# An attention and expert-retrieval block: x of 16 tokens copied earlier, five rounds of row gathers ahead of the scatter, gates stored in quarters

## The chip, the cores and the metric

The kernel runs on one core of a Trainium2 chip. A core has TensorE (PE; its weight loads are PEld), VectorE (DVE), ScalarE (ACT), GpSimd (POOL), the SP sequencer that only issues DMAs here, and 16 DMA engines. Every engine runs its own program in order, and the programs meet at semaphores. The metric is the device time of one execution in microseconds (us); less is better.

## The reference

One block of 512 tokens of width 1024, all in float32:

```
z   = x @ w_in                       # attention: two groups of 8 heads
x1  = layer_norm(ALPHA * x + concat(fox(z), swa(z)) @ w_out)
q   = x1 @ w_pq                      # 8 heads, two halves of 128
v1, i1 = top16(q_a . keys1);  v2, i2 = top16(q_b . keys2)
sc, pos = top16(all 256 sums v1 + v2)      # 16 experts a head of 128 * 128
gate = softmax(sc);  e = i1 * 128 + i2
w   = gelu(u_tab[e] . x1) * gate           # 8 heads * 16 = 128 experts a token
out = layer_norm(ALPHA * x1 + sum(w * v_tab[e]))
```

## The kernel before

**Precision.** A float32 product is made of three passes of rounded parts: hi*hi, lo*hi and hi*lo. Each 128 x 1024 tile of a table is loaded into one of four `raw` slots by SP, rounded to `hi` by ScalarE (`split_hi`, L446), and the rest is made by GpSimd (`split_lo`, L452). There are four such pairs for expert tiles. SP loads tile c + 4 only when the `lo` of tile c is made.

**Tokens.** The 512 tokens are four blocks of 128. Blocks 1 to 3 (384 columns, `DENSE`) are computed densely: TensorE multiplies x1 with all 128 tiles of u (L1806 to L1808), ScalarE takes the gelu (L1018), the result is stored to DRAM as `gelu_scratch` (L557), the last 12 tiles being kept on chip. Then weights = gelu * gate enter the products with the 128 tiles of v (L1861 to L1863). Block 0 is done by gathers: GpSimd gathers for each of 128 ranks the row of u of every token (L765) and VectorE takes the dot with x1 (L1347). The dots run against a copy of x in PSUM, `x1_home`, that ScalarE writes with `home` (L1047). Eight ranks make a round; there are eight row buffers, so rank k is gathered only when the dot of rank k - 8 is done (`row_used`). The last 16 tokens of block 3 are also left out of the dense u product (368 columns): their 16 * 128 rows are spread over all 128 partitions as 16 more ranks, the "late" ones. For these, SP copies numbers (L580), gates (L587) and x (L592) of the 16 tokens across partitions, eight DMAs each, and later brings the weights back (L598).

**The route.** VectorE finds the chosen experts block by block (`route_block`), with dots in the gaps (`DOT_GAPS`), 28 in all; after the gate sums it does dots until `R_PRE` rounds of eight are done (`while done[0] < R_PRE * ROWS`), then casts the gates and begins the one-hots.

**The scatter.** The gates of the dense tokens must be laid out by expert. For eight tokens at a time VectorE makes one-hot rows (L1570, L1577, L1578), TensorE multiplies them (L2078, L2079) and ScalarE copies the result to one of two `stage` buffers (L1060). A chunk is 32 tokens, four such groups, six u tiles; `two_chunks(o)` covers twelve u tiles, and there are six of them, o = 0 to 5. Ahead of them are 44 u tiles (`A_PRE`, numbers 0 to 43), behind them 12. After the sixth and the twelfth tile of a pair SP stores a whole stage buffer (2 MB, L610), and ScalarE waits for that store (`g_stored`) before it writes the buffer again. In the first pair the scatters stand after tiles 2 to 5 (numbers 46 to 49) and then after each (0, 1, 3, 4) of six.

**Orders that the change touches.** ScalarE, first pair: gelu of tile 44, `take_turned`, gelu of tile 45, wait for the copies of x and for `R_PRE * ROWS` dots, `home(late_x)`, gelu of tile 46, copy of group 0, and so on. After the first pair: wait for all late dots, `home(x1)`, gelu of the late dots. GpSimd: with `split_first` a tile is split and then the gathers wait for their dots; without, the waits of the tile's ranks come ahead of its split. SP, in the first pair: numbers ahead of it, gates and x after its first tile, weights after its last. In `finish_norm` (L1283) the root is awaited (L1285), then four small operations follow (L1286 to L1290), then the product with the gain (L1295) and the last one with the bias. At the end ScalarE rounds weights 125 and 126, the last v tile, weight 127, and GpSimd splits the last eight v tiles with no wait of its own; VectorE subtracts for the weights (L1683).

The two waits around which the text turns:

```
act.wait_ge(late_x_moved, 16 * SPREAD)
act.wait_ge(row_used, R_PRE * ROWS)
home(late_x)
```

## Time and profile before

| | us |
|---|---|
| median of 3 runs | 1469.04 |
| lowest, highest | 1467.37, 1470.72 |
| the profiled execution's own time | 1468.22 |
| its span | 1466.5 |
| TensorE busy in it | 1427.7 |

The span goes from the first to the last instruction of the profiled execution; the time of an execution is 1.7 us longer than the span. All times in rows are microseconds from the span's start. In a timeline a row has start and duration, engine and line (of the kernel before), the operation, output<-input, the shapes, how many are merged, and in square brackets how long the engine idled ahead of it and what ended that. SPq is SP issuing DMAs. A full clock is 1.00, a half one 0.50.

### The profile page before, as it was taken

To read this page: it belongs to the slowest core of one execution; us is meant where nothing else is said; L and a number is where in the kernel's file an instruction comes from. 1 tells how busy PE (TensorE), PEld (TensorE's weight loads), DVE (VectorE), ACT (ScalarE), POOL (GpSimd) and SP (SyncE) were. 2 spreads that over 40 slices of the span, in tenths; PEclk is the share of its full clock that TensorE was granted. 3 is DMA by queue.
4 is the path that set the end of the run, shared out by engine and by line. 5 is a ranking of instruction groups with operands and counts; after the bars stand their busy time and mean duration, and the time that the engine had idled before them with its cause. 6 is when DMAs were issued, how large, how long until landed. Compare 5 with 4: busy or idle time off the path is not lost.

```text
span 1466.5 us, 25059 instructions
## 1 busy us (share of the span) xinstructions
PE 1427.7 (97%) x8029; PEld 1268.8 (87%) x8029; DVE 1031.7 (70%) x2204; ACT 608.6 (41%) x1018; POOL 1014.2 (69%) x631
## 2 busy tenths in 40 slices
PE   9999999999999987999999999999999999999996
PEld 5888888889999977999999999888888888888875
DVE  5466665788999958999887594765555555555587
ACT  5666741334333334444444443333333333333332
POOL 3332321435698856788788689988888888888885
PEclk9999999999999998999999999999999999999998
DMA  6212211324699858899999899999999999999981
GB/s 237 73 59 101 78 68 37 107 86 137 188 348 325 297 200 300 347 406 413 393 386 365 315 411 382 359 396 365 352 357 353 363 355 343 352 354 348 354 328 57
DMA packets 136906, 406.95 MB, mean 277 GB/s; under 512 B 13904, under 2 KB 56656, under 8 KB 134672
## 3 DMA queue, kind: packets, MB, share of 16 engines
q1 hardware_dynamic: 97088, 263.48, 49.5%
q0 software_dynamic: 39760, 142.76, 25.1%
q8 instruction: 29, 0.48, 0.1%
q14 instruction: 29, 0.24, 0.0%
HBM read 355.50 MB, written 50.14 MB: 277 GB/s over the span
## 4 chain that ended last, share of the span: by engine, by line
PE 86%; DVE 5%; ACT 2%; issue 2%; POOL 2%; SPq 2%; DMA 1%; POOLq 0%; DVEq 0%; ACTq 0%
PE banks L1806 14%; PE banks L1808 14%; PE banks L1807 14%; PE banks L1861 12%; PE banks L1863 12%; PE banks L1862 12%; PE banks L1923 2%; PE banks L2078 1%; PE banks L2079 1%; DVE rows L1347 1%; POOL lo L452 1%; PE banks L2015 1%; PE banks L1907 1%; DVE gate_lo L1578 1%; DVE is_i L1570 1%
## 5 line engine op out<-in xcount | busy, mean ns | idle before, releaser
L452 POOL TENSOR_TENSOR lo<-raw,hi 128x1024 fp32r<-128x1024 f32 x292 | 703.5, 2410 | 352.3 <-ACT hi L446 337.3
L1806 PE MATMUL banks<-x1T_hi,hi 128*128 128x368 f32 (+3 forms) x1168 | 396.2, 339 | 2.5 <-ACT gelu L1018 1.7
L1807 PE MATMUL banks<-x1T_lo,hi 128*128 128x368 f32 (+3 forms) x1168 | 390.7, 335 | 0.0
L1808 PE MATMUL banks<-x1T_hi,lo 128*128 128x368 f32 (+3 forms) x1168 | 390.4, 334 | 0.0
L446 ACT ACTIVATE hi<-raw 128x1024 fp32r<-128x1024 f32 x292 | 306.9, 1051 | 30.9 <-DMA raw<-u_t 18.1
L1861 PE MATMUL banks<-hi,wgt_hi 128*128 128x512 f32 x750 | 291.9, 389 | 1.2 <-DVE wgt_lo L1683 1.2
L1862 PE MATMUL banks<-lo,wgt_hi 128*128 128x512 f32 x750 | 291.8, 389 | 0.0
L1863 PE MATMUL banks<-hi,wgt_lo 128*128 128x512 f32 x750 | 291.8, 389 | 0.0
L1683 DVE TENSOR_TENSOR wgt_lo<-wgt,wgt_hi 128x384 fp32r<-128x384 f32 x125 | 89.6, 718 | 201.0 <-ACT wgt_hi L1101 105.1
L1806 PEld LDWEIGHTS banks<-x1T_hi,hi 128*128 128x128 f32 x1168 | 219.9, 188 | 7.3 <-issue 2.7
L1808 PEld LDWEIGHTS banks<-x1T_hi,lo 128*128 128x128 f32 x1168 | 219.7, 188 | 4.4
L1807 PEld LDWEIGHTS banks<-x1T_lo,hi 128*128 128x128 f32 x1168 | 220.0, 188 | 3.9
L1101 ACT ACTIVATE wgt_hi<-wgt 128x384 fp32r<-128x384 f32 x125 | 65.6, 525 | 318.2 <-PE banks L1863 308.1
L1347 DVE CUSTOM_DVE_ANT_0 rows<-rows,banks 128x1024 f32<-128x1024 f32 x144 | 170.6, 1214 | 36.1 <-DMA rows<-u_rows,expert_at 20.1
L1861 PEld LDWEIGHTS banks<-hi,wgt_hi 128*128 128x128 f32 x750 | 140.8, 188 | 30.8 <-DVE wgt_lo L1683 1.7
L1863 PEld LDWEIGHTS banks<-hi,wgt_lo 128*128 128x128 f32 x750 | 140.8, 188 | 29.4
L1018 ACT ACTIVATE gelu<-banks 128x368 f32<-128x368 f32 x116 | 55.4, 478 | 266.9 <-PE banks L1808 232.1
L1862 PEld LDWEIGHTS banks<-lo,wgt_hi 128*128 128x128 f32 x750 | 140.8, 188 | 29.1
L1715 DVE SCALAR_TENSOR_TENSOR banks<-rows,row_weight,banks 128x1024 f32<-128x1024 f32 x128 | 164.0, 1281 | 0.7
L765 POOL DMA_INDIRECT rows<-u_rows,expert_at x144 | 140.0, 972 | 28.6 <-issue 22.4
L765 POOL DMA_INDIRECT rows<-v_tab,expert_at x128 | 126.3, 987 | 20.0 <-issue 7.5
L1570 DVE TENSOR_TENSOR is_i<-banks,selT 128x1024 f16<-128x1024 f16 x92 | 59.2, 684 | 19.0 <-remote 13.6
(231 smaller groups left out, 1758.0 us busy)
## 6 DMA issues: line engine op xcount, KB each, us to landing
raw<-u_t SPq DMA_DIRECT2D x128, 512.0 KB
raw<-v_tab SPq DMA_DIRECT2D x128, 512.0 KB
g_scratch<-stage SPq DMA_DIRECT2D x12, 2048.0 KB
gelu_scratch<-gelu SPq DMA_DIRECT2D x116, 192.0 KB
ga<-gelu_scratch SPq DMA_DIRECT2D x29, 768.0 KB
gg<-g_scratch SPq DMA_DIRECT2D x14, 1536.0 KB
raw<-w SPq DMA_DIRECT2D x26, 512.0 KB
raw<-w_pq SPq DMA_DIRECT2D x16, 512.0 KB
```

Source lines behind the costliest of these rows:

```text
L446: act.activation(parts_of(c)[0][:, :], raw[:, c % RAW_SLOTS, :], ACT.Copy).then_inc(hi_ready, 1)
L452: eng.tensor_tensor(l[:, :], raw[:, c % RAW_SLOTS, :], h[:, :].bitcast(F32), ALU.subtract).then_inc(lo_ready, 1)
L765: pool.indirect_dma_start(rows[:, k % ROWS, :], None, table, at).then_inc(gathered[k % ROWS], 16)
L1347: dve.tensor_tensor_reduce(rows[:, k, :], rows[:, k, :], x1_home, 1.0, 0.0, ALU.mult, ALU.add, dots8[:, k:k + 1]).then_inc(row_used, 1)
L1683: dve.tensor_tensor(l[:, :], wgt[k % 2][:, :], h[:, :].bitcast(F32), ALU.subtract).then_inc(wgt_lo_ready, 1)
L1715: dve.scalar_tensor_tensor(y0, rows[:, k, :], row_weight[:, bass.ds(ROWS * r + k, 1)], y0, ALU.mult, ALU.add).then_inc(row_used, 1)
L1806: pe.matmul(o, h[:, s], hiT[:, k, tokens], start=(k == 0), stop=False)
L1807: pe.matmul(o, h[:, s], loT[:, k, tokens], start=False, stop=False)
L1808: ins = pe.matmul(o, l[:, s], hiT[:, k, tokens], start=False, stop=(k == KT - 1))
L1861: pe.matmul(o, h_at(b), h[:, s], start=start, stop=False)
L1862: pe.matmul(o, h_at(b), l[:, s], start=False, stop=False)
L1863: ins = pe.matmul(o, l_at(b), h[:, s], start=False, stop=stop)
```

## The change

- `late_x` gets a buffer of its own beside the routing's, and its eight copies leave right after the load of the keys. It was a view of `sel`.
- `R_PRE` is 5, not 4: gathers move forward one tile each from tile 25 on, and ranks 36 to 39 are gathered at tiles 44 to 47. The last pair then has eight dots, not sixteen.
- A stage buffer is stored as four pieces of 32 expert tiles (512 KB each), one behind each of four loads, beginning with the tile after the half's last one.
- The numbers leave two tiles earlier, the gates three tiles later; the weights are brought back after the second pair, and the late dots end (`late_dots_done`) at the second tile of the second pair on ScalarE; VectorE waits for that home after its first one-hots of that pair.
- The exp of the scores stands ahead of four gelus, not two.
- GpSimd waits for weight 119's parts ahead of its last eight splits; ScalarE rounds the last v tile ahead of weight 126; in `finish_norm` the product with the gain stands ahead of the wait for the root.

```diff
@@ -81,6 +81,7 @@
 O_MID = CHUNKS // 2
+STORE_PARTS = 4
 A_PRE = 44
@@ -88,16 +89,18 @@
 A_POST = ETILES - A_PRE - A_MID
-R_PRE = 4
-R_MID = 2 * O_MID
+R_PRE = 5
+R_MID = 2 * O_MID - 1
 R_LATE = LATE_RANKS // ROWS
...
 AHEAD = 4
-FIRST_ROWS_AT = (13, 13, 14, 15, 15, 16, 17, 17, 18, 19, 19, *range(20, 25), *range(26, 30),
-                 *range(31, 35), *range(36, 44))
+FIRST_ROWS_AT = (13, 13, 14, 15, 15, 16, 17, 17, 18, 19, 19, *range(20, 32), 32, 32, *range(33, 44),
+                 44, 45, 46, 47)
 assert len(FIRST_ROWS_AT) == R_PRE * ROWS
+MID_ROWS = (2, 1, 1) * (MID_TILES // 3)
 LATE_ROWS = (0, 0, 0, 0, 3, 3, 3, 3, 2, 2, 2, 2)
+LAST_MID_ROWS = (1, 1, 0) * (MID_TILES // 3)
 assert sum(LATE_ROWS) == LATE_RANKS + AHEAD
@@ -223,7 +226,6 @@
         row_weight = sb("row_weight", [P, RANKS])
-        late_x = sel[:, 0:2, :, :].rearrange("p m b n -> p (m b n)")
         block_numbers = row_weight[:, :].bitcast(U32)
@@ -242,6 +244,7 @@
         gsum = sb("gsum", [P, 2, TB * PH], F32, route)
+        late_x = sb("late_x", [P, D], F32, route)
         route.close()
@@ -547,6 +550,12 @@
             sp.dma_start(keys[:, :, :], keys_t).then_inc(keys_loaded, 16)
+
+            def late_group(g):
+                return slice(LATE_TOKENS * g, LATE_TOKENS * (g + 1))
+
+            for g in range(SPREAD):
+                sp.dma_start(late_x[late_group(g), :], x1[LATE_AT:, TB - 1, :]).then_inc(late_x_moved, 16)
             with sp.Fori(1, LISTS // 4) as i:
@@ -566,13 +575,6 @@
             sp.wait_ge(ones_ready, GELU_SLOTS)
-            with sp.Fori(0, A_PRE // 4) as it:
-                for k in range(4):
-                    store_and_load(k, it)
-
-            def late_group(g):
-                return slice(LATE_TOKENS * g, LATE_TOKENS * (g + 1))
-
             def move_numbers():
@@ -580,17 +582,13 @@
                                  block_numbers[LATE_AT:, late_group(g)]).then_inc(late_numbers_moved, 16)
-            def move_gates_and_x():
+            def move_gates():
                 sp.wait_ge(gates_ready, 1)
...
                                  sel[LATE_AT:, 2, TB - 1, late_group(g)]).then_inc(late_gates_moved, 16)
-                sp.wait_ge(sel_turned, 2)
-                for g in range(SPREAD):
-                    sp.dma_start(late_x[late_group(g), :], x1[LATE_AT:, TB - 1, :]).then_inc(late_x_moved, 16)
-
             def move_weights():
@@ -598,21 +596,36 @@
                                  late_weight[late_group(g), :]).then_inc(late_weight_moved, 16)
+            def store_gates(o, half, part):
+
+                if part == 0:
+                    sp.wait_ge(staged, 4 * GROUPS_PER_CHUNK * o + 2 * GROUPS_PER_CHUNK * (half + 1))
+                rows_of = slice(part * ETILES // STORE_PARTS, (part + 1) * ETILES // STORE_PARTS)
+                sp.dma_start(g_dram[2 * o + half, :, rows_of, :], stage[half][:, rows_of, :]).then_inc(g_stored[half], 16)
+
             def two_chunks(o, first=False):
...
                     store_and_load(t % 4, 3 * o + (A_PRE // 4 + t // 4))
-                    if first and t == 0:
-                        move_gates_and_x()
-                    if t % (MID_TILES // 2) == MID_TILES // 2 - 1:
-                        half = t // (MID_TILES // 2)
-
-                        sp.wait_ge(staged, 4 * GROUPS_PER_CHUNK * o + 2 * GROUPS_PER_CHUNK * (half + 1))
-                        sp.dma_start(g_dram[2 * o + half], stage[half][:, :, :]).then_inc(g_stored[half], 16)
-
+                    if first and t == 3:
+                        move_gates()
+
+                    if t < STORE_PARTS and not first:
+                        store_gates(o - 1, 1, t)
+                    if MID_TILES // 2 <= t < MID_TILES // 2 + STORE_PARTS:
+                        store_gates(o, 0, t - MID_TILES // 2)
+
+            with sp.Fori(0, A_PRE // 4 - 1) as it:
+                for k in range(4):
+                    store_and_load(k, it)
+            for k in range(2):
+                store_and_load(k, A_PRE // 4 - 1)
             move_numbers()
+            for k in range(2, 4):
+                store_and_load(k, A_PRE // 4 - 1)
             two_chunks(0, first=True)
+            two_chunks(1)
             move_weights()
-            with sp.Fori(1, O_MID) as o:
+            with sp.Fori(2, O_MID) as o:
                 two_chunks(o)
@@ -624,14 +637,15 @@
                              ).then_inc(comb_loaded[slot], 16)
-            for k in range(A_PRE + A_MID + 8, ETILES):
+            for n, k in enumerate(range(A_PRE + A_MID + 8, ETILES)):
                 load_tile(sp, S_U + k, 0, u_t[k])
+                store_gates(O_MID - 1, 1, n)
             for slot in range(GELU_SLOTS):
...
             for half in range(2):
-                sp.wait_ge(g_stored[half], 16 * CHUNKS // 2)
+                sp.wait_ge(g_stored[half], 16 * STORE_PARTS * CHUNKS // 2)
             load_group(KEPT_FROM, 0)
@@ -765,13 +779,15 @@
                     pool.indirect_dma_start(rows[:, k % ROWS, :], None, table, at).then_inc(gathered[k % ROWS], 16)
+            def first_rows(k):
+                return [n for n, tile in enumerate(FIRST_ROWS_AT) if tile == k]
+
             for k in range(A_PRE):
...
                     pool.wait_ge(expert_ready, 1)
-                ranks = [n for n, tile in enumerate(FIRST_ROWS_AT) if tile == k]
-                gather(u_rows, ranks, 0, (S_U + k, 0), split_first=True)
-
-            def some_rows(first, r, tile, it, counts=(2, 1, 1) * (MID_TILES // 3)):
+                gather(u_rows, first_rows(k), 0, (S_U + k, 0), split_first=True)
+
+            def some_rows(first, r, tile, it, counts=MID_ROWS):
                 n = first
@@ -780,9 +796,16 @@
                     gather(u_rows if own_rows else v_rows, ranks, r, (tile + t, it))
-            some_rows(R_PRE * ROWS, 0, S_U + A_PRE, 0, LATE_ROWS)
-            with pool.Fori(1, O_MID) as o:
+            n = R_PRE * ROWS
+            for t in range(MID_TILES):
+                k = A_PRE + t
+                ranks = [*first_rows(k), *range(n, n + LATE_ROWS[t])]
+                n += LATE_ROWS[t]
+                gather(u_rows, ranks, 0, (S_U + k, 0))
+            with pool.Fori(1, O_MID - 1) as o:
                 some_rows(R_PRE * ROWS + AHEAD, 2 * o, S_U + A_PRE, 3 * o)
+            last = R_PRE + 2 * (O_MID - 1)
+            some_rows(last * ROWS + AHEAD, 0, S_U + A_PRE + A_MID - MID_TILES, 0, LAST_MID_ROWS)
             some_rows((R_PRE + R_MID) * ROWS + AHEAD, 0, S_U + A_PRE + A_MID, 0)
@@ -796,6 +819,7 @@
                 gather(v_rows, [U_ROWS + ROWS * LAST_OCTET + AHEAD + n for n in asked], 0, (N_TILES - 16 + k, 0))
+            pool.wait_ge(wgt_lo_ready, ETILES - 8)
             for k in range(8):
@@ -1025,11 +1049,9 @@
                     gelu_tile(k, it)
-            for k in range(2):
-                gelu_tile(k, A_PRE // 4 - 1)
             act.wait_ge(route_step, ROUTE_STEPS * (TB - 1) + SCORE_STEPS)
             act.activation(sel[:, 2, :, :], sel[:, 2, :, :], ACT.Exp).then_inc(gate_exp, 1)
-            for k in range(2, 4):
+            for k in range(4):
                 gelu_tile(k, A_PRE // 4 - 1)
@@ -1054,14 +1076,21 @@
                     if tile == 0 and g == 0 and not first:
-                        act.wait_ge(g_stored[chunk_half], 16 * o)
+                        act.wait_ge(g_stored[chunk_half], 16 * STORE_PARTS * o)
                     t0 = tile * TOK_PER_TILE + 4 * g
...
                                    ACT.Copy, scale=scale).then_inc(staged, 1)
-            def two_chunks(o, first=False, last=False):
+            def late_dots_done():
+
+                act.wait_ge(row_used, (R_PRE + R_LATE) * ROWS)
+                home(x1[:, 0, :])
+                act.wait_ge(dots8_free, R_PRE + R_LATE + 1)
+                act.activation(late_gelu, late_dots, ACT.Gelu).then_inc(late_gelu_ready, 1)
+
+            def two_chunks(o, first=False, second=False, last=False):
                 for half in range(2):
@@ -1073,7 +1102,9 @@
                             act.wait_ge(row_used, R_PRE * ROWS)
-                            home(late_x)
+                            home(late_x[:, :])
+                        if second and tile == 1:
+                            late_dots_done()
                         if t in after:
@@ -1082,12 +1113,8 @@
             two_chunks(0, first=True)
-
-            act.wait_ge(row_used, (R_PRE + R_LATE) * ROWS)
-            home(x1[:, 0, :])
-            act.wait_ge(dots8_free, R_PRE + R_LATE + 1)
-            act.activation(late_gelu, late_dots, ACT.Gelu).then_inc(late_gelu_ready, 1)
-            with act.Fori(1, O_MID - 1) as o:
+            two_chunks(1, second=True)
+            with act.Fori(2, O_MID - 1) as o:
                 two_chunks(o)
@@ -1118,8 +1145,8 @@
             weight_hi(ETILES - 3, 0, True)
+            split_hi(act, N_TILES - 1, 0)
             weight_hi(ETILES - 2, 0, True)
-            split_hi(act, N_TILES - 1, 0)
             weight_hi(ETILES - 1, 0, True)
@@ -1281,6 +1308,9 @@
             def finish_norm(b, n, gb=None, done=None):
+                if gb is not None:
+                    chained(dve.scalar_tensor_tensor(sums(b), sums(b), moments[:, b, 0:1], gb[:, 0, :],
+                                                     ALU.subtract, ALU.mult))
                 dve.wait_ge(sqrt_ready, n + 1)
@@ -1292,8 +1322,6 @@
                     return
-                chained(dve.scalar_tensor_tensor(sums(b), sums(b), moments[:, b, 0:1], gb[:, 0, :],
-                                                 ALU.subtract, ALU.mult))
                 if n < TB:
@@ -1624,7 +1652,7 @@
             one_hots(0, 0, True)
-            def two_chunks(o, first, last=False):
+            def two_chunks(o, first=False, second=False, last=False):
                 for tile in range(8):
@@ -1633,21 +1661,23 @@
                         dve.wait_ge(homes_ready, 3)
-                    for n in (2 * tile, 2 * tile + 1):
+                    if second and tile == 0:
+                        dve.wait_ge(homes_ready, 4)
+                    for n in ((tile,) if last else (2 * tile, 2 * tile + 1)):
                         dot(n % ROWS, 2 * o + (R_PRE + n // ROWS))
...
                             keep_dots(2 * o + (R_PRE + n // ROWS))
-            two_chunks(0, True)
+            two_chunks(0, first=True)
+            two_chunks(1, second=True)
             dve.wait_ge(late_gelu_ready, 1)
...
             dve.tensor_tensor(late_weight, late_gelu, late_gates, ALU.mult).then_inc(late_weight_ready, 1)
-            dve.wait_ge(homes_ready, 4)
-            with dve.Fori(1, O_MID - 1) as o:
-                two_chunks(o, False)
+            with dve.Fori(2, O_MID - 1) as o:
+                two_chunks(o)
             late_in_parts()
-            two_chunks(O_MID - 1, False, last=True)
+            two_chunks(O_MID - 1, last=True)
             def weights(k, i, j, par):
@@ -1689,8 +1719,8 @@
                 keep_dots(r)
-            dve.wait_ge(g_stored[0], 16 * CHUNKS // 2)
-            dve.wait_ge(g_stored[1], 16 * CHUNKS // 2)
+            dve.wait_ge(g_stored[0], 16 * STORE_PARTS * CHUNKS // 2)
+            dve.wait_ge(g_stored[1], 16 * STORE_PARTS * CHUNKS // 2)
             dve.wait_ge(ones_ready, GELU_SLOTS + 1)
```

## Rows read from the trace of the kernel before

**Rows 1.** The page, part 1: busy time and share of each engine.

```profile
PE 1427.7 (97%) x8029; PEld 1268.8 (87%) x8029; DVE 1031.7 (70%) x2204; ACT 608.6 (41%) x1018; POOL 1014.2 (69%) x631
```

**Rows 2.** TensorE's waits: total us, times, longest.

```profile
PE banks L2078 <- ACT stage L1060: 15.9, 2, 15.2
...
PE banks L1806 <- ACT gelu L1018: 1.7, 1, 1.7
...
PE banks L1861 <- DVE wgt_lo L1683: 1.2, 1, 1.2
...
PE banks L1976 <- DVE x L1298: 0.6, 1, 0.6
```

**Rows 3.** Timeline of TensorE at scatters 0 and 1: start, duration, [idle before].

```profile
538.45 0.23 PE L2078 MATMUL banks<-gate_hi,is_i 128*128 128x128 f16 x1
...
558.76 0.27 PE L2078 MATMUL banks<-gate_hi,is_i 128*128 128x128 f16 x1 [15.19 <-ACT stage L1060]
```

**Rows 4.** Timeline of ScalarE, at `home(late_x)`.

```profile
555.77 1.03 ACT L1047 ACTIVATE banks<-sel 128x1024 f32<-128x1024 f32 x1 [19.70 <-DMA sel<-x]
```

**Rows 5.** Timeline of the SP queue, the copies of x.

```profile
544.31 5.02 SPq L592 DMA_DIRECT2D sel<-x  x8
```

**Rows 6.** Windows: busy PE, PEld, DVE, ACT, POOL, clock, DMA share, GB/s.

```profile
546.00:547.00 1.00, 0.00 (x0) 0.00 (x0) 0.00 (x0) 0.00 (x0) 0.69 (x2) 0.94 1.03 338
...
563.00:564.00 1.00, 1.00 (x5) 1.00 (x5) 1.00 (x3) 0.00 (x0) 0.69 (x2) 0.53 0.91 323
```

**Rows 7.** Timeline of VectorE, gate sums to first one-hots.

```profile
520.29 0.69 DVE L1537 TENSOR_REDUCE gsum<-sel 128x32 f32<-128x512 f32 x1 [3.09 <-ACT sel L1031]
...
522.01 1.21 DVE L1347 CUSTOM_DVE_ANT_0 rows<-rows,banks 128x1024 f32<-128x1024 f32 x1
...
532.17 0.36 DVE L1546 CAST gate_half<-selT 128x384 f16<-128x384 f32 x1 [5.32 <-ACT selT L1040]
...
533.75 1.29 DVE L1570 TENSOR_TENSOR is_i<-banks,selT 128x1024 f16<-128x1024 f16 x2
```

**Rows 8.** Timeline of VectorE, two successive one-hots.

```profile
564.86 1.28 DVE L1570 TENSOR_TENSOR is_i<-banks,selT 128x1024 f16<-128x1024 f16 x2
...
570.60 1.28 DVE L1570 TENSOR_TENSOR is_i<-banks,selT 128x1024 f16<-128x1024 f16 x2
```

**Rows 9.** Timeline of GpSimd: tile 44's split, and the last u gather.

```profile
514.39 2.40 POOL L452 TENSOR_TENSOR lo<-raw,hi 128x1024 fp32r<-128x1024 f32 x1 [0.50 <-ACT hi L446]
...
910.94 0.96 POOL L765 DMA_INDIRECT rows<-u_rows,expert_at  x1 [0.16 <-issue]
```

**Rows 10.** Timeline of VectorE, the dot of that last gather.

```profile
917.46 1.22 DVE L1347 CUSTOM_DVE_ANT_0 rows<-rows,banks 128x1024 f32<-128x1024 f32 x1 [1.57 <-DMA rows<-u_rows,expert_at]
```

**Rows 11.** Timeline of ScalarE in chunk 2, tiles 59 and 60.

```profile
619.05 1.06 ACT L446 ACTIVATE hi<-raw 128x1024 fp32r<-128x1024 f32 x1 [0.52 <-DMA raw<-u_t]
...
629.08 0.48 ACT L1018 ACTIVATE gelu<-banks 128x368 f32<-128x368 f32 x1 [8.00 <-DMA gelu_scratch<-gelu]
```

**Rows 12.** Timeline of the SP queue, moved weights and a steady load.

```profile
613.11 0.34 SPq L434 DMA_DIRECT2D raw<-u_t  x1
...
613.97 8.49 SPq L598 DMA_DIRECT2D dots_gelu<-small  x8
...
765.25 0.35 SPq L434 DMA_DIRECT2D raw<-u_t  x1
```

**Rows 13.** Timeline of ScalarE, V's first tile and U's last.

```profile
924.05 1.06 ACT L446 ACTIVATE hi<-raw 128x1024 fp32r<-128x1024 f32 x1 [2.86 <-DMA raw<-v_tab]
...
930.95 0.48 ACT L1018 ACTIVATE kept<-banks 128x368 f32<-128x368 f32 x1 [1.45 <-PE banks L1808]
```

**Rows 14.** Timeline of GpSimd, two of the last splits.

```profile
1412.50 4.74 POOL L452 TENSOR_TENSOR lo<-raw,hi 128x1024 fp32r<-128x1024 f32 x2
```

**Rows 15.** Timeline of VectorE, the subtractions near the end.

```profile
1413.38 4.29 DVE L1683 TENSOR_TENSOR wgt_lo<-wgt,wgt_hi 128x384 fp32r<-128x384 f32 x1
...
1439.32 3.22 DVE L1683 TENSOR_TENSOR late_lo<-wgt,late_hi 128x384 fp32r<-128x384 f32 x2
```

## The prediction

> **What bounds the kernel now.** I read the page first: TensorE is busy for 97% of the span [rows 1], so time can only come out of its idle 39 us, or out of stretches at the lower clock. The waits of TensorE name most of that idle time [rows 2]: one wait of 15.2 for a gate copy of ScalarE, and small ones of 0.7, 1.7, 1.2 and 0.6. TensorE's timeline places the long one [rows 3]: scatter 0 starts at 538.45, and scatter 1 starts at 558.76 after 15.19 idle, so TensorE stopped at 543.57. ScalarE's timeline tells why [rows 4]: it sat 19.70 us ahead of `home(late_x)` for the copies of x; the scatter's results are copied by the same ScalarE further down its program. The SP queue issues those eight copies only from 544.31 to 549.33 [rows 5], behind `gates_ready`, the eight copies of gates and `sel_turned`. The windows give the clock [rows 6]: full speed until 546.9 (3.4 us into the stall), half speed until 563.95 (5.2 us after the restart). 5.2 us at half speed lose 2.6.
>
> **Part by part.**
>
> *x of the 16 tokens early.* The copies move to the load of the keys (252 us). They need x1 alone. SP issues eight more DMAs, some 5 us by the pace of rows 5, ahead of the fifth w_pq tile, which ScalarE rounds only at 265; it may land 7 us after issue without harm. Cost 0, at most 1. The 15.19 stall loses its cause, so the question is what is late next.
>
> *Exp two tiles earlier.* VectorE idled 3.09 for the exp before the gate sums [rows 7]. Its input is there early, so the gates are ready at about 518.9, not 522.0 (the first dot starts at 522.01). ScalarE has idle time between tiles that hides the two table loads: cost 0.
>
> *Five rounds before the scatter.* VectorE now owes twelve dots there, not four. The pitch of a dot is 1.14 (of the 5.74 from 564.86 to 570.60 [rows 8], two dots take 2.3 and the one-hots of a tile 3.46). Ranks 36 to 39 are gathered at tiles 44 to 47, and there GpSimd waits for a dot *before* it splits. Tile 44's split stood at 514.39 [rows 9]; rank 36 needs dot 28, which ends at 520.1. Each of four turns is 2.40 (split) + 0.96 (gather) + 0.2 = 3.55, so the gathers are issued by 523.7, 527.2, 530.7 and 534.3. (TensorE needs tile 44's parts at 524.7; they are there at 522.5: covered, with 2 us to spare.) The landing isn't shown for a quiet queue. In a full one, the gather issued at 910.94 to 911.90 [rows 9] was used at 917.46 after a wait [rows 10]: 5.6. From below it is 0; I take 4.0, as DMA is half idle here. The last row is there at 538.2, its dot ends at 539.4, the casts of the gates take 1.6 (532.17 to 533.75 [rows 7]), the one-hots 3.6: scatter 0 can start at 544.8, not 538.45. So a stall of 6.3 (4.5 to 8) takes the place of 15.19. The Trainium skill's "DMA: Bandwidth & Descriptors", Specifications, gives a first byte after about 1 us for GpSimd's DMAs and 435 GB/s for the fabric; by that 512 KB land in an estimated 2.2 us and the sum would be 1.8 better. No row here shows it.
>
> *Numbers and gates of the 16 tokens.* The numbers' eight copies now follow tile 41's store and load; that load waits for the split of tile 45 (526.1), so they are issued by 531.4 and landed at about 533. GpSimd wants them at tile 48, at 534.3, and split tile 48 at 536.5 before: nothing is later. The stores of tiles 42 and 43 come 5 us later on SP, four tiles ahead of their need. The gates' eight copies stand behind tile 47's load; what SP has next waits for GpSimd's split of tile 52 (565) anyway. Cost 0 (2 at most, if a load behind them lands late).
>
> *Clock.* 6.3 is longer than 3.4, so I let the clock fall again and lose the same 2.6. Scatter 1 then starts at 544.8 + 5.1 (scatter 0 and tile 47, as from 538.45 to 543.57) + 2.6 = 552.5, against 558.76 + 2.6 = 561.4: **8.9 gained**. If the clock stays up, VectorE is next (one-hots each 5.74, against 4.97 for tile and scatter) and only 1.1 more comes.
>
> *Late dots finished in the second pair of chunks.* `home(x1)` now stands behind tile 57's gelu. In the old run tile 59 ended at about 618.0 (its split of the next tile starts at 619.05 after 0.52 idle and the gelu's 0.48 [rows 11]), so tile 57 ended at 618.0 - 4.0 - 4.97 = 609.0. Less 8.9 that is 600.1; gelu 0.4, split 1.05 and home 1.03 end at 602.6; two dots (2.3) at 604.9; only then does GpSimd split tile 59, until 607.4. TensorE wants it at 600.1 + 0.97 + 4.0 = 605.1. New stall: **2.3 lost** (0 to 5).
>
> *Gates in four pieces.* The bytes are the same, in pieces that let loads pass. But the last piece leaves three tiles later, and the buffer is written again sooner. In steady state a load is issued 4.9 after its tile's gelu (765.25 [rows 12]) and the buffer is written about 10 after that; ScalarE may be 3 late before TensorE feels it. A 512 KB load issued at 613.11 was used at 619.05 [rows 11, 12]: 5.9, so a piece behind it lands in some 8: covered in steady state. In the second pair SP runs 12 us behind the gelus because GpSimd's splits wait for dots; there I count 0.8 and 1.5: **2.3 lost** (0 to 6). What this and the moved weights remove: at 613.97 SP spent 8.49 on eight copies [rows 12], the gelu store behind them landed at 629, ScalarE had waited 8.00 for it [rows 11] and TensorE 1.7, then 0.7 [rows 2]. A pair later SP isn't late and the store has 5 us more: **2.4 gained**.
>
> *Last pair with eight dots; V's start.* VectorE gets 9 us free, where it isn't the bound: 0. At the end the four pieces go out with the last four loads, and SP waits for the last one before the gates' reads and V's first tile. That tile is already late: ScalarE waited 2.86 for it until 924.05, TensorE wants its parts at 930.95 [rows 13]. 1.05 + 2.4 after 924.05 leave 3.4 us. Waiting for a piece moves it by 3 (0 to 7): 0 counted, 3.6 at worst.
>
> *GpSimd's wait before the last eight splits.* Its two splits ran 1412.50 to 1417.24 [rows 14]; VectorE's subtraction of two SBUF operands, normally 0.56, took 4.29 from 1413.38 [rows 15], and TensorE waited 1.2 for it [rows 2]. The new wait puts the splits behind it; they have a tile of slack. **1.2 gained**. *The swap on ScalarE at the end* goes the other way: the rounding of weight 126 now follows the last tile's rounding (1438.5 to 1439.5), so its subtraction comes when GpSimd's last split runs. Of the two in 3.22 [rows 15] the first escaped and the second was held; now both are: **0.6 lost**. The Trainium skill's "SBUF — State Buffer", section on two separate sides, says that VectorE with two SBUF inputs and GpSimd exclude each other for a whole instruction. The trace agrees (4.29 against 0.56), and by that rule too this swap can't gain.
>
> *Norm edit.* The product with the gain fills the wait for the square root in the one block where TensorE waits 0.6 for x [rows 2]: **0.3 gained** (0 to 0.6); at the end GpSimd's chain ends as late, so nothing.
>
> **Sum.** 8.9 - 2.3 - 2.3 + 2.4 + 1.2 - 0.6 + 0.3 = 7.6. The profiled execution took 1468.2 (span 1466.5); it stands 0.8 under the median 1469.04. Less 7.6: 1460.6, and as a median **1461.4**.
>
> **Rivals.**
> - *More comes.* Gathers land fast, pieces land in time, GpSimd's dots don't hold tile 59: 7.6 + 1.8 + 2.3 + 2.3, less a little, is 13: 1456. For it: DMA at 0.3 to 0.5 share about 530. Against: the order of ScalarE's program is fixed. Chance 0.28.
> - *The new stall before scatter 0 eats it.* If a gather takes 8 or GpSimd's turns slip by a split's 2.4 each, scatter 0 starts at 551 and 6 of the 7.6 go: 1467.5. For it: VectorE must do twelve dots and the one-hots in one string. Chance 0.10.
> - *Slower: the stage buffers.* They are reused ten times. With DMA at a share of 1.0 from 650 on, a piece that lands 14 after issue, not 8, passes the 10 + 3 by 1.2, ten times 1.2 is 12, and V's start adds 3: 1461.4 + 12 = 1473 to 1476. It decides as soon as the landing passes 13.7. For it: ScalarE waited 8.00 for a store once [rows 11]. Against: that was behind a 2 MB store, which is gone. Chance 0.12.
> - Forecast 0.50, own range 1458 to 1465.
>
> About 0.2% (2.9 us) can be told from no change. Faster: 0.5 + 0.28 + a little of the second rival = 0.79; same 0.10; slower 0.11. Range for 8 in 10: 1455.0 to 1467.8.
>
> **What would show it.** TensorE's longest wait becomes one at scatter 0 (L2078 released by VectorE's `gate_lo`), 4.5 to 8 us, with half clock behind it; no wait for ScalarE's `home`; a wait of 1 to 5 at tile 59 for GpSimd's `lo`; ScalarE's waits for `g_scratch<-stage` only in the second pair. The last split of 4.29 becomes under 1. I am wrong if the stall at scatter 0 is under 3 or above 9, if ScalarE waits for pieces in every pair, or if TensorE stops at V's start.

## The result, and the profile after

The changed kernel takes **1477.63 us** (median of 6 runs, 1476.67 to 1479.74) against 1469.36 (6 runs on the same chip): ratio **1.006**, 95% interval 1.0048 to 1.0072. It is 8.3 us slower; 1461.4 was forecast, with a range up to 1467.8. Its profiled execution has a span of 1475.7, 9.2 over that of before. One of the 17 runs of the kernel before that stand beside the first group of experiments took 4245.63 us, and the ratios leave it out.

Part 1 of the page, which answers to [rows 1]:

```profile
PE 1431.1 (97%) x8029; PEld 1272.0 (86%) x8029; DVE 1033.6 (70%) x2204; ACT 608.3 (41%) x1018; POOL 1014.2 (69%) x631
```

TensorE does the same 8029 matmuls and is busy 3.4 us longer; the other 5.8 of the 9.2 are more idle time. Its waits (total us, times, longest), which answer to [rows 2]:

```profile
PE banks L2108 <- ACT stage L1082: 10.5, 2, 6.5
PE banks L2108 <- DVE gate_lo L1606: 9.7, 1, 9.7
...
PE banks L1836 <- POOL lo L455: 2.2, 4, 0.9
PE banks L1836 <- ACT kept L1042: 2.1, 2, 1.5
PE banks L1891 <- DVE late_lo L1713: 1.6, 1, 1.6
...
PE banks L1891 <- DVE wgt_lo L1713: 0.8, 1, 0.8
...
PE banks L2006 <- DVE x L1326: 0.3, 1, 0.3
```

The one long stall of before has become three. TensorE's timeline (start, duration, idle before) places them:

```profile
548.06 0.29 PE L2108 MATMUL banks<-gate_hi,is_i 128*128 128x128 f16 x1 [9.74 <-DVE gate_lo L1606]
...
606.97 0.23 PE L2108 MATMUL banks<-gate_hi,is_i 128*128 128x128 f16 x1 [3.98 <-ACT stage L1082]
...
644.35 0.29 PE L2108 MATMUL banks<-gate_hi,is_i 128*128 128x128 f16 x1 [6.54 <-ACT stage L1082]
```

The first is the stall at scatter 0 that took the place of the 15.19 of [rows 3]. The other two are new, and both belong to the second pair of chunks. ScalarE's timeline shows what it waited for just before each:

```profile
606.32 1.08 ACT L1082 ACTIVATE stage<-banks 128x512 f32<-128x512 f32 x2 [6.83 <-DMA g_scratch<-stage]
...
643.70 1.08 ACT L1082 ACTIVATE stage<-banks 128x512 f32<-128x512 f32 x2 [5.59 <-DMA g_scratch<-stage]
```

It may not write a stage buffer before the buffer's last piece has landed. When these pieces left is in the timeline of the SP queue:

```profile
579.96 0.56 SPq L604 DMA_DIRECT2D g_scratch<-stage  x1
...
596.29 0.43 SPq L604 DMA_DIRECT2D g_scratch<-stage  x1
...
619.81 0.43 SPq L604 DMA_DIRECT2D g_scratch<-stage  x1
...
631.70 0.50 SPq L604 DMA_DIRECT2D g_scratch<-stage  x1
```

The first piece of a buffer leaves at 579.96, the fourth at 596.29, since three tiles' loads and stores stand between. ScalarE wants the buffer at 606.32 - 6.83 = 599.5, but the piece lands 10.0 after its issue. In the other half it leaves at 631.70 and has landed 12.0 later; ScalarE wanted that buffer at 643.70 - 5.59 = 638.1.

The start of V is late too. The last piece of all leaves at 910.41, and SyncE, which must see it landed, reads the first gates only at 920.42, 10.0 later. TensorE stops for `kept` (0.61, then 1.51) and for `wgt_lo` (0.78 at 948.84), 2.9 in all:

```profile
935.61 0.44 PE L1836 MATMUL banks<-x1T_hi,hi 128*128 128x368 f32 x1 [1.51 <-ACT kept L1042]
```

Windows of after (busy PE, PEld, DVE, ACT, POOL, clock, DMA share, GB/s), one of each stretch at the lower clock, answer to [rows 6]:

```profile
549.00:550.00 1.00, 1.00 (x10) 1.00 (x9) 1.00 (x2) 0.61 (x2) 0.00 (x0) 0.50 1.02 414
...
608.00:609.00 1.00, 1.00 (x9) 1.00 (x8) 0.00 (x0) 1.00 (x2) 0.00 (x0) 0.50 0.07 25
...
646.00:647.00 1.00, 1.00 (x6) 1.00 (x4) 1.00 (x3) 1.00 (x3) 0.83 (x1) 0.50 1.03 421
```

Slices of 1 us put the half clock (0.50, the 1.2 GHz level) behind each restart at 548.06 to 552.5, 607.2 to 610.6 and 644.35 to 648.1: 4.5, 3.4 and 3.8 us, half of which is lost, 5.9 in all against 2.6 before. These 3.3 are the longer busy time.

So the 9.2 are accounted for, but for some tenths: the long stall has 5.4 less, the stage buffers 10.5 - 0.7 = 9.8 more, `gelu` 1.7 less, `lo` 0.8, `kept` 2.1 and `late_lo` 1.4 more, `wgt_lo` 0.4 less (1.24 near the end gone, 0.78 at V's start new), `x` 0.3 less, the clock 3.3 more, which makes 9.6.

### The profile page after: what moved, and what is told of

Its sections match the earlier page's. It is cut to its first block, busy times and chain, and to the rows that moved or that the text cites. A ratio compares the mean times of both kernels' runs of the same rounds, so it can differ in the third digit from the quotient of the medians.

```text
span 1475.7 us, 24931 instructions
## 1 busy us (share of the span) xinstructions
PE 1431.1 (97%) x8029; PEld 1272.0 (86%) x8029; DVE 1033.6 (70%) x2204; ACT 608.3 (41%) x1018; POOL 1014.2 (69%) x631
## 4 chain that ended last, share of the span: by engine, by line
PE 81%; DVE 7%; POOL 4%; DMA 3%; issue 3%; ACT 2%; SPq 0%; DVEq 0%; ACTq 0%; POOLq 0%
PE banks L1836 13%; PE banks L1838 12%; PE banks L1837 12%; PE banks L1891 12%; PE banks L1892 12%; PE banks L1893 12%; POOL lo L455 3%; PE banks L1953 2%; DMA g_scratch<-stage 1%; PE banks L2108 1%; PE banks L2109 1%; DVE rows L1375 1%; PE banks L2045 1%; POOL rows L779 1%; DMA raw<-v_tab 1%
## 5 line engine op out<-in xcount | busy, mean ns | idle before, releaser
L449 ACT ACTIVATE hi<-raw 128x1024 fp32r<-128x1024 f32 x292 | 306.8, 1051 | 15.6 <-DMA raw<-v_tab 6.6
L1713 DVE TENSOR_TENSOR wgt_lo<-wgt,wgt_hi 128x384 fp32r<-128x384 f32 x125 | 86.2, 690 | 196.7 <-ACT wgt_hi L1128 106.2
```

Of the source, the lines that this page charges most:

```text
L449: act.activation(parts_of(c)[0][:, :], raw[:, c % RAW_SLOTS, :], ACT.Copy).then_inc(hi_ready, 1)
L1713: dve.tensor_tensor(l[:, :], wgt[k % 2][:, :], h[:, :].bitcast(F32), ALU.subtract).then_inc(wgt_lo_ready, 1)
```

## The experiments

Each time is a median on the same chip beside runs of the kernel before (1469.57, 1469.89 and 1469.07 in the three groups: e1, e2, b1, b3; then c1 to c4; then d1 to d5). Ratios are to those. The medians of before differ by 0.8 between groups, so a difference between runs of two groups is no surer than that. Diffs are cut; `...` marks where.

**e1_whole and e2_at_once: how the stores leave.** Both are the changed kernel. In e1_whole each gate buffer leaves as one store again, after the sixth and the twelfth tile of a pair:

```diff
-STORE_PARTS = 4
+STORE_PARTS = 1
...
-                    if t < STORE_PARTS and not first:
-                        store_gates(o - 1, 1, t)
-                    if MID_TILES // 2 <= t < MID_TILES // 2 + STORE_PARTS:
-                        store_gates(o, 0, t - MID_TILES // 2)
+                    if t % (MID_TILES // 2) == MID_TILES // 2 - 1:
+                        for part in range(STORE_PARTS):
+                            store_gates(o, t // (MID_TILES // 2), part)
...
-                store_gates(O_MID - 1, 1, n)
```

e2_at_once has the same edit with `STORE_PARTS = 4`: four pieces, one right after the other.

> The changed kernel, but each stage buffer leaves whole (one 2 MB store) after the sixth and the twelfth tile of a pair, as before. Theory 1 (the four pieces leave too late, so ScalarE waits 6.8 and 5.6 us for them in the second pair, TensorE 4.0 + 1.0 and 6.5, each with a fall of the clock, and 2.9 more at V's start): those waits go, 14 to 19 us less than the changed kernel, 1459 to 1464, with at most 2 us of the old wait behind the store. Rival (the twelve dots ahead of the scatter are what costs): at most 3 us less, 1475 or more.

> The changed kernel with four pieces, all four issued one behind the other where the whole store stood (after the sixth and the twelfth tile of a pair). Theory 1 (when they leave counts, not that they are four): within 2 us of the kernel with whole stores, 1459 to 1465. Rival (four DMAs with 4 KB a partition cost more than one with 16 KB): nearer to the changed kernel, 1472 or more.

Measured: e1_whole 1465.02, ratio 0.997 (0.9961 to 0.998), 1.0 above the range of its theory; e2_at_once 1464.8, ratio 0.9972 (0.9961 to 0.9983). The number of pieces costs nothing that can be seen; spreading them over tiles costs 12.6 us. Without it the change is a gain of 4.5. What differs is when the buffer is on its way as a whole. In e1_whole it leaves at 574.54, where the changed kernel's last piece leaves at 596.29. Timeline of the SP queue:

```profile
574.54 0.43 SPq L604 DMA_DIRECT2D g_scratch<-stage  x1
```

The store's own landing is no shorter: in e1_whole a whole store of 2 MB takes 8.7 to 14.7 (median 11.3), and in e2_at_once a piece takes 5.3 to 15.6 (median 10.8). TensorE's timeline of e1_whole shows what is left:

```profile
548.56 0.29 PE L2106 MATMUL banks<-gate_hi,is_i 128*128 128x128 f16 x1 [10.25 <-DVE gate_lo L1604]
...
611.00 0.43 PE L1834 MATMUL banks<-x1T_hi,hi 128*128 128x368 f32 x1 [2.38 <-POOL lo L455]
...
636.77 0.23 PE L2106 MATMUL banks<-gate_hi,is_i 128*128 128x128 f16 x1 [1.02 <-ACT stage L1080]
```

**b3_pieces and b1_x_early: one part of the change alone, on the kernel before.** b3_pieces has the four spread pieces and nothing else. b1_x_early has x copied at the load of the keys, into the buffer of its own, and nothing else:

```diff
-        late_x = sel[:, 0:2, :, :].rearrange("p m b n -> p (m b n)")
...
+        late_x = sb("late_x", [P, D], F32, route)
...
             sp.dma_start(keys[:, :, :], keys_t).then_inc(keys_loaded, 16)
...
+            for g in range(SPREAD):
+                sp.dma_start(late_x[late_group(g), :], x1[LATE_AT:, TB - 1, :]).then_inc(late_x_moved, 16)
...
-                sp.wait_ge(sel_turned, 2)
-                for g in range(SPREAD):
-                    sp.dma_start(late_x[late_group(g), :], x1[LATE_AT:, TB - 1, :]).then_inc(late_x_moved, 16)
```

> The kernel before with one part of the change: the stage buffers leave in four pieces, one behind each of four loads. Theory 1: ScalarE waits for pieces in the second pair as in the changed kernel, and SP is later still there, as it moves the weights then: 8 to 18 us slower than before, 1477 to 1487. Rival (pieces only hurt where the five rounds leave no room): 1468 to 1472.

> The kernel before with one part of the change: x of the 16 tokens in a buffer of its own, copied right behind the load of the keys; four rounds ahead of the scatter, whole stores, all else as before. Theory 1: the wait of 15.2 and its 2.6 of half clock go and no stall takes their place at scatter 0; the late gathers, issued from 539, make VectorE wait a few us instead: 1453 to 1460. Rival (only five rounds ahead let the gain come, since the first late dot must wait for its gather): a new stall of 8 or more near scatter 2 or 3, 1463 or more.

Measured: b3_pieces 1484.7, ratio 1.0102 (1.0085 to 1.0119), 15 us slower; b1_x_early **1457.73**, ratio 0.9922 (0.9906 to 0.9939), 12 us faster. In b3_pieces the 15.22 of scatter 1 is there as before, and behind it:

```profile
612.41 0.23 PE L2086 MATMUL banks<-gate_hi,is_i 128*128 128x128 f16 x1 [2.88 <-ACT stage L1068]
...
646.23 0.23 PE L2086 MATMUL banks<-gate_hi,is_i 128*128 128x128 f16 x1 [4.19 <-ACT stage L1068]
...
877.04 0.27 PE L2086 MATMUL banks<-gate_hi,is_i 128*128 128x128 f16 x1 [5.86 <-ACT stage L1068]
```

In b1_x_early the stall is cut to one short wait and some smaller ones, and the `gelu` wait of [rows 2] stays:

```profile
550.90 0.23 PE L2077 MATMUL banks<-gate_hi,is_i 128*128 128x128 f16 x1 [2.28 <-DVE gate_lo L1577]
...
618.14 0.43 PE L1805 MATMUL banks<-x1T_hi,hi 128*128 128x368 f32 x1 [1.99 <-ACT gelu L1017]
```

Moving x is worth 12 us by itself, more than the whole change was forecast to bring. The changed kernel with whole stores is still 7.3 slower than x alone, so something beside the pieces loses too.

**c1_x_wait_norm and c2_plus_swap: the end.** c1 is b1_x_early with GpSimd's wait and the norm edit; c2 adds the swap on ScalarE:

```diff
+            pool.wait_ge(wgt_lo_ready, ETILES - 8)
             for k in range(8):
                 split_lo(pool, N_TILES - 8 + k, 0)
```

```diff
+            split_hi(act, N_TILES - 1, 0)
             weight_hi(ETILES - 2, 0, True)
-            split_hi(act, N_TILES - 1, 0)
```

> The kernel before with three parts of the change: x of the 16 tokens copied early into a buffer of its own, GpSimd's wait before its last eight splits, and the norm edit on VectorE. The rounds, the order of SyncE, the whole stores and the order on ScalarE at the end are those of before. My theory (what the run with x alone showed, 1457.7, and what the prediction priced for the two small edits): TensorE's 1.24 us wait on weight_lo near the end goes, 0.3 us comes from the norm, so about 1456.2 (1455.2 to 1457.2). Rival: the early splits of GpSimd were hidden and its wait only hands the lateness to the last splits (TensorE waits for POOL lo in the last eight tiles): 1457.7 or more.

> As c1_x_wait_norm, and on ScalarE split_hi of the last tile stands ahead of weight_hi of tile 126, as in the changed kernel. The theory from the traces: TensorE's last wait on late_lo is 1.62 us with the swap (in the changed kernel and in both runs made from it) and 0.19 without, since the swap makes VectorE's weight_lo of tile 126 late by one ScalarE instruction: 1.0 to 1.4 us slower than c1_x_wait_norm, about 1457.4. Rival: the 1.62 come from VectorE's own order and not from the swap: no difference within 0.5 us, and a wait of 0.2 us in the trace.

Measured: 1456.77 (ratio 0.9904, 0.9887 to 0.9922) and 1456.79 (0.9911, 0.9894 to 0.9929). c1 gains 1.0 on b1_x_early, which the intervals don't separate. The swap makes no difference in time that four runs of each can show: the rival of c2 was right on that, and wrong on the wait. TensorE's wait on `late_lo` was 0.19 before; it is 0.92 in c1 and 1.62 in c2. Timeline of c1, then of c2:

```profile
1432.96 0.47 PE L1862 MATMUL banks<-hi,late_hi 128*128 128x512 f32 x1 [0.92 <-DVE late_lo L1684]
```

```profile
1430.78 0.47 PE L1862 MATMUL banks<-hi,late_hi 128*128 128x512 f32 x1 [1.62 <-DVE late_lo L1684]
```

So GpSimd's wait removes 1.24 and gives 0.7 back at the last tile, and the swap adds another 0.7 to the wait there, too little to see in the medians.

**c3_two_parts: the dose.** The changed kernel with two pieces, at the tiles where the first two of four were.

> The changed kernel with each store of the gates in two pieces of 1 MB, one a tile, rather than four: the first leaves where it left, the last two tiles (about 9 us) earlier. Theory (a piece that leaves late holds the stage buffer, ScalarE waits for it and TensorE for ScalarE; with four pieces ScalarE waits 6.8 and 5.6 us in the second pair): with 9 us less both waits go but for 1 us, TensorE's 3.98 and 6.54 us too, and the time is 1464 to 1468. Rival (a store between two loads costs for itself, since it delays the loads behind it in SyncE's order, however many pieces there are): 1473 or more, with waits for ScalarE or GpSimd that stay over 5 us.

Measured: 1470.44 (1466.89 to 1471.44), ratio 0.9997 (0.9986 to 1.0007): between 1465.0 (whole) and 1477.6 (four), and between the two forecasts. The list of ScalarE's waits has none for a stage buffer any more, as my theory had it, but TensorE still stops there:

```profile
612.79 0.43 PE L1837 MATMUL banks<-x1T_hi,hi 128*128 128x368 f32 x1 [4.02 <-POOL lo L455]
...
641.49 0.29 PE L2109 MATMUL banks<-gate_hi,is_i 128*128 128x128 f16 x1 [3.96 <-ACT stage L1083]
```

ScalarE's timeline says what had taken the place of the wait for the buffer:

```profile
599.60 0.48 ACT L1043 ACTIVATE gelu<-banks 128x368 f32<-128x368 f32 x1 [3.96 <-DMA gelu_scratch<-gelu]
...
637.43 0.48 ACT L1043 ACTIVATE gelu<-banks 128x368 f32<-128x368 f32 x1 [4.40 <-DMA gelu_scratch<-gelu]
```

The gelu store that the first of them waits for is issued at 587.05, right behind the second piece of 1 MB (586.00), and lands 12.5 later. Timeline of the SP queue:

```profile
587.05 0.49 SPq L566 DMA_DIRECT2D gelu_scratch<-gelu  x1
```

So the theory (only the last piece's departure counts) holds for the buffer and is incomplete for the time. That the piece delays what is issued behind it fits this order, but isn't shown by itself: with whole stores ScalarE waits for gelu stores too, 6.7 at most in e2_at_once, and there TensorE has no stall over 2.4 but the one at scatter 0.

**c4_four_rounds and d4_four_rounds_pieces: the fifth round.** c4 is e1_whole, d4 the changed kernel, both with four rounds at the places of before:

```diff
-R_PRE = 5
-R_MID = 2 * O_MID - 1
+R_PRE = 4
+R_MID = 2 * O_MID
...
-                    for n in ((tile,) if last else (2 * tile, 2 * tile + 1)):
+                    for n in (2 * tile, 2 * tile + 1):
```

> The changed kernel with whole stores (as e1_whole, 1465.0) and with four rounds of gathers before the scatter rather than five, at the places of before; the last pair computes 16 dots again. All else is the change's: x early, the order of SyncE, tile 59's dots, the end. Theory: the fifth round is what makes VectorE late for scatter 0, since its last dot waits for the gather of rank 39 (5.9 us idle); without it TensorE's 10.25 us wait falls to about 2.3 us as in the run with x alone, and the time is 1457 to 1460. Rival: the later place of the tokens' numbers and dots (tile 59, TensorE's 2.4 us) and the end cost what e1_whole loses against x alone, and the fifth round little: 1463 or more.

> The changed kernel with four rounds of gathers rather than five; the four pieces stay. With c4_four_rounds 1454.4, e1_whole 1465.0 and the changed kernel 1477.6 it completes a square of rounds by stores. If the two losses are separate (10.6 for the fifth round, 12.6 for the pieces): 1467.0 (1465.5 to 1468.5), faster than before; TensorE waits for stage in the second pair over 8 us in all. Rival: the pieces hurt as much as they do only because the fifth round made the kernel late there (or the early start makes the stores collide more): under 1464, or over 1470.

Measured: c4 **1454.43**, ratio 0.989 (0.9872 to 0.9908), below the 1457 to 1460 of its theory; d4 1474.41 (1472.16 to 1476.11), ratio 1.0033 (1.0022 to 1.0043). With whole stores the fifth round costs 10.6 us, and without it the stall at scatter 0 is gone. With pieces it costs only 3.2, and the pieces cost 20.0 in four rounds against 12.6 in five: the losses don't add. The time that d4 was expected to take was wrong and its rival (over 1470) came true, though TensorE does wait over 8 for `stage` in the second pair (9.65), as was expected. TensorE's timeline of d4:

```profile
595.74 0.23 PE L2106 MATMUL banks<-gate_hi,is_i 128*128 128x128 f16 x1 [3.32 <-ACT stage L1080]
...
634.46 0.29 PE L2106 MATMUL banks<-gate_hi,is_i 128*128 128x128 f16 x1 [6.33 <-ACT stage L1080]
...
864.98 0.26 PE L2106 MATMUL banks<-gate_hi,is_i 128*128 128x128 f16 x1 [5.28 <-ACT stage L1080]
```

The stall in the last pair of chunks is in b3_pieces and d4, both of four rounds, and not in the changed kernel, whose last pair gathers 8 rows fewer. In d4 the last piece of that buffer leaves 8.7 ahead of ScalarE's need and lands 13.2 after its issue. Timeline of the SP queue, then of ScalarE:

```profile
851.02 0.33 SPq L604 DMA_DIRECT2D g_scratch<-stage  x1
```

```profile
864.23 1.08 ACT L1080 ACTIVATE stage<-banks 128x512 f32<-128x512 f32 x2 [4.48 <-DMA g_scratch<-stage]
```

So the fifth round pays something back there. Which of the fewer gathers and fewer dots does it wasn't separated.

**d3_last_gather_earlier: the stall at scatter 0.** e1_whole with the last four gathers at other tiles:

```diff
-                 44, 45, 46, 47)
+                 44, 45, 45, 46)
```

> e1_whole (1465.0: the changed kernel with whole stores), with the last four gathers before the scatter at tiles 44, 45, 45, 46 rather than 44 to 47, so that the last is issued about 2.3 us earlier. Theory: VectorE's dots before the scatter end when the last gather has landed (7.0 us after its issue in the changed kernel, not the 4.0 that the prediction took), and TensorE's 10.25 us wait follows it: about 7.9 us, the time 1462.5 (1461.5 to 1463.7). Rival: VectorE is late by its twelve dots themselves, whatever the gathers do, or the earlier gathers land later behind SyncE's loads: no difference within 0.7 us.

Measured: **1460.44**, ratio 0.994 (0.9923 to 0.9956), 4.6 faster than e1_whole, better than the theory. GpSimd's timeline, then VectorE's and TensorE's:

```profile
530.84 0.95 POOL L777 DMA_INDIRECT rows<-u_rows,expert_at  x1 [0.16 <-issue]
```

```profile
535.74 1.22 DVE L1373 CUSTOM_DVE_ANT_0 rows<-rows,banks 128x1024 f32<-128x1024 f32 x1 [0.57 <-DMA rows<-u_rows,expert_at]
```

```profile
543.74 0.29 PE L2106 MATMUL banks<-gate_hi,is_i 128*128 128x128 f16 x1 [5.45 <-DVE gate_lo L1604]
```

The same lines of the changed kernel:

```profile
533.21 0.96 POOL L779 DMA_INDIRECT rows<-u_rows,expert_at  x1 [0.16 <-issue]
```

```profile
541.15 1.22 DVE L1375 CUSTOM_DVE_ANT_0 rows<-rows,banks 128x1024 f32<-128x1024 f32 x1 [5.88 <-DMA rows<-u_rows,expert_at]
```

The last gather leaves 2.4 earlier and its row is used 5.4 earlier: 3.9 us behind the end of the issue, not 7.0. In e1_whole, from which d3 differs by this edit alone, the gather leaves at 533.13 and its row is used at 541.82, 7.7 behind the end of the issue. In the changed kernel it comes behind a burst of SyncE, which had stood still for eight small copies:

```profile
526.37 5.30 SPq L582 DMA_DIRECT2D small<-row_weight  x8
531.71 0.58 SPq L566 DMA_DIRECT2D gelu_scratch<-gelu  x1
532.33 0.43 SPq L437 DMA_DIRECT2D raw<-u_t  x1
```

In d3 the burst begins at 532.14, after the gather's 530.84. That the burst is what made it late fits both traces; taking the burst away was not tried. The three gathers before the last one landed 5.4, 4.6 and 3.4 behind the end of their issue in the changed kernel, so the landing varies by some us there in any case.

**d1_late_dots_between and d5_best: the best version.** d1 is c4 with `home(x1)` between the pairs, where it was before; d5 undoes the swap as well.

```diff
-                        if second and tile == 1:
-                            late_dots_done()
...
-            two_chunks(1, second=True)
+            late_dots_done()
+            two_chunks(1)
```

> As c4_four_rounds (1454.4), and ScalarE puts x1 home for the dots of the second pair between the pairs, as in the kernel before, rather than behind the gelu of tile 57. In c4_four_rounds VectorE idles 7.34 us before the second pair's first dot, its dots being done at 583.9, and TensorE waits 2.38 us for GpSimd's lo of tile 59. Theory: both go, 2 to 2.4 us, about 1452.2 (1451.5 to 1453.2). Rival: the same lateness comes back as the wait for the gelu store or the stage (1.8 to 2 us, as in c1_x_wait_norm at 617.8): 1454 or more.

> d1_late_dots_between with ScalarE's order at the end as in the kernel before (weight_hi of tile 126 ahead of split_hi of the last tile). It is the version that all runs so far point to: x early, four rounds, whole stores, the tokens' numbers and weights at their later places, GpSimd's wait, the norm edit. Theory: 0 to 0.7 us faster than d1_late_dots_between (TensorE's wait on late_lo 0.9 rather than 1.6, as c1 against c2, where the times were equal), about 1451.8. Rival: the order at the end is worth nothing within 0.5 us either way.

Measured: d1 **1448.9** (1448.44 to 1449.84), ratio 0.9861 (0.9845 to 0.9878); d5 1449.24 (1448.79 to 1449.97), ratio 0.9864 (0.9848 to 0.9881). Both beat both kernels, by 20 us that of before. d1 gains 5.5 on c4 where 2 to 2.4 were expected. TensorE's timeline of c4 shows the two stalls that it had there:

```profile
599.78 0.44 PE L1832 MATMUL banks<-x1T_hi,hi 128*128 128x368 f32 x1 [2.38 <-POOL lo L455]
...
624.82 0.23 PE L2104 MATMUL banks<-gate_hi,is_i 128*128 128x128 f16 x1 [1.86 <-ACT stage L1078]
```

d1 has neither, and differs from c4 by this edit alone, so the second wait was an echo of GpSimd's lateness at tile 59. ScalarE's timeline of c4 has a step of its way, which goes through SyncE's loads and stores for the tiles behind:

```profile
612.36 0.48 ACT L1038 ACTIVATE gelu<-banks 128x368 f32<-128x368 f32 x1 [5.87 <-DMA gelu_scratch<-gelu]
```

The two waits are 4.2. The second one also lowered the clock, as the windows of c4 show (columns as above), and TensorE is busy 1426.1 us in c4 and 1424.2 in d1, which is another 1.9:

```profile
625.00:626.00 1.00, 1.00 (x18) 0.96 (x16) 1.00 (x1) 0.62 (x2) 0.70 (x2) 1.00 1.02 420
626.00:627.00 1.00, 1.00 (x6) 1.00 (x6) 1.00 (x4) 0.99 (x2) 0.98 (x2) 0.64 1.01 402
...
628.00:629.00 1.00, 1.00 (x5) 1.00 (x4) 1.00 (x2) 0.04 (x1) 0.84 (x2) 0.50 1.21 497
```

Against these 6.1 stands a wait of 0.6 for `kept` in d1: 5.5, beside 5.1 between the two spans (1453.3 and 1448.2) and 5.5 between the medians of two groups. As between c1 and c2, the swap is worth nothing that can be seen in time.

## Why the prediction was wrong

By its own steps:

- *x early, 15.19 loses its cause.* Right: `home(late_x)` waits for no DMA, and the part alone brings 12 us.
- *Five rounds before the scatter.* The mechanism was right: a stall at scatter 0, released by `gate_lo`. The size was not: 9.74 measured against 6.3 (range 4.5 to 8). The working's own terms make scatter 0 start at 539.4 + 1.6 + 3.6 = 544.6, not the 544.8 written, which changes little. The term that failed is the landing of the last gather: 4.0 taken "as DMA is half idle here", 7.0 measured. The row in a full queue [rows 9, 10] said 5.6, and the half-idle share was that of the old kernel, in which the eight small copies and SyncE's burst behind them stood elsewhere: from 534 to 541 it is 0.23 before and 0.98 after. The change itself moved them beside this gather. d3 measured 3.9 with the gather ahead of the burst. 8.9 should have been 8.9 - 3.0 = 5.9, and tile 56's gelu did come 6.1 earlier (598.07 against 604.20).
- *And the wrong comparison.* The 8.9 were credited to the change as a whole. I noted that VectorE now owes twelve dots rather than four, yet never priced the fifth round by itself. c4 against e1_whole does: it costs 10.6. The gain was x (12 us alone); with whole stores the round took most of it back.
- *Clock.* Right for this stall: it fell 4 us into the idle time and lost 2.2. It was counted for one stall; two more fell with it.
- *Late dots in the second pair.* 2.3 was forecast, and 2.38 is what tile 59 shows in e1_whole. In the changed kernel itself the stall for the stage buffer stands ahead of it, and no wait for `lo` is over 0.9. The echo behind it and the clock were not counted: with four rounds and whole stores d1 puts the whole step at 5.5.
- ***Gates in four pieces*: this step turned the sign.** I counted 2.3 lost (0 to 6); the difference to e1_whole is 12.6. The steps were the right ones (the last piece leaves three tiles later, SP is late in the second pair), but the landing was read as 8 by adding to a load's 5.9 [rows 11, 12]. It was 10.0 and 12.0, and the waits 3.98 and 6.54 where I had 0.8 and 1.5. Had the pieces landed in 8, these waits would still have been an estimated 2.0 and 2.5 (3.98 less 2.0, 6.54 less 4.0), so the rest of the miss is in how soon ScalarE wants the buffer. Two stalls that long also pull the clock down twice (3.6). That the steady pairs cover the piece was right here, in the changed kernel alone; with four rounds the last pair didn't.
- *V's start: 0 counted, 3.6 at worst.* TensorE waits 2.9 there, 2.1 for `kept` and 0.8 for `wgt_lo`, since SyncE waits 10.0 for the last piece; e1_whole shows one wait of 0.47. The forecast had named a stop at V's start, and a stall at scatter 0 above 9 (it was 9.74), as signs that it was wrong, and both came.
- *The rival that came true* is the stage buffers, given 0.12. I let it decide at 13.7 us of landing, in all ten uses, from the slack of a steady pair. In the second pair ScalarE wants the first buffer 3.2 us after its last piece is issued, so there any landing above about 6 (with the 3 us that ScalarE may be late) decided. The threshold was put in the wrong place of the program. Its own figures don't agree either: a landing of 14 passes 10 + 3 by 1.0, not 1.2, and no term gives the 13.7. That its 1473 to 1476 lies near the measured 1477.6 is luck: two long stalls made most of the loss, not ten of 1.2.
- *Moved weights, whole store: 2.4 gained.* The waits of 1.7 and 0.7 are gone, as forecast, but e1_whole has 1.02 in their place.
- *GpSimd's wait, swap, norm.* 1.2 - 0.6 + 0.3 was forecast. The wait for `wgt_lo` near the end is gone and that for `x` fell from 0.6 to 0.3, but `late_lo` grew by 1.4, not 0.6: the sum is 0.1. With a split of GpSimd beside them (1448.10 to 1450.82), VectorE's two subtractions on `late_lo` take 3.20, against 0.55 for the one before them. The Trainium skill's "SBUF — State Buffer", section on two separate sides, says that a VectorE instruction with two SBUF inputs and one of GpSimd that reads SBUF take turns at a shared pair of ports, each holding it for its whole length. The trace agrees. Timeline of VectorE in the changed kernel, which answers to [rows 15]:

```profile
1447.45 0.55 DVE L1713 TENSOR_TENSOR late_lo<-wgt,late_hi 128x384 fp32r<-128x384 f32 x1
...
1448.51 3.20 DVE L1713 TENSOR_TENSOR late_lo<-wgt,late_hi 128x384 fp32r<-128x384 f32 x2
```

- *Exp earlier, numbers and gates: 0.* The exp did what it was meant to: the first dot is at 518.70, 3.3 earlier. What that brings in time no run separates. The numbers' copies were costed by their own landing alone; what came behind them in the queue met the gather.

With 7.0 for the gather and the measured waits and clock of the pieces the same sum would read 5.9 - 2.3 - 10.5 - 3.6 + 2.4 + 0.1 = -8.0, or 1468.2 + 8.0 + 0.8 = 1477.0. That this is so near 1477.6 is in part luck: the 2.3 is not in the changed kernel's trace, where waits for `lo` grew by 0.8, and the 2.9 at V's start are left out. With these two it is -9.4, against the 9.2 of the spans. Two DMA landings were taken too short. The gather's lies in a stretch that the change made busier (0.23 to 0.98). The pieces' lie in stretches that were full before as well: the DMA share is 1.00 from 596.3 to 606.3 and 1.05 from 631.7 to 643.7 in the kernel before, and 1.03 in both after.

## What to carry to other kernels

When a transfer is split to let others pass, price the moment at which its *last* part leaves and lands, at the place where the queue is latest and not in steady state, and then what stands behind each part. When a change makes room in a tight place and at once fills it again (x out, a fifth round in), price the two apart: here the first alone was worth 12 us, and the second cost 10.6. Removing the cause of a short stall (2.38) brought 5.5, since the delay came back through SyncE's program order and lowered the clock as well.

## What the runs showed of the hardware

- Size alone didn't say when a DMA lands. The last gather ahead of scatter 0 was used 3.9 us behind its issue in d3 and 7.0 in the changed kernel, where it left 2.4 us later. Pieces of 512 KB landed 10.0, 12.0 and 13.2 after issue, with DMA at a share of 1.03 in each of these stretches, and the whole stores of 2 MB in e1_whole after 8.7 to 14.7.
- Four stores of 512 KB issued together cost the same as one of 2 MB (1464.8 and 1465.0).
- TensorE's clock fell for short stalls too: 3.98 us of idle time were followed by 3.4 us at half, so the stall took 5.7 us in all. In c4 the stall of 1.86 at 624.82 was followed by half clock from 626.3 to 629.7, while the one of 2.38 at 599.78 was not (the clock is 1.00 in each slice from 599 to 605). In e1_whole a stall of the same 2.38, at 611.00, was followed by half clock from 611.4 to 614.8. So the length of a stall alone doesn't say whether the clock falls. A window of e1_whole (columns as above):

```profile
612.00:613.00 1.00, 1.00 (x5) 1.00 (x5) 1.00 (x3) 0.00 (x0) 0.69 (x2) 0.50 0.83 156
```
